# Expert sums of a decoder step: picked rows gathered per token in place of dense scoring and summing

## The reference, cut to what matters

```python
q = (hx @ w_pq).reshape(PEER_BLOCK, PEER_HEADS, 2, PK_HALF)
s = jnp.einsum('nhpc,hpkc->nhpk', q, sub_keys).astype(jnp.float32)
top_s, top_i = lax.top_k(s, PEER_TOPK)
cand = top_s[:, :, 0, :, None] + top_s[:, :, 1, None, :]
best_s, best = lax.top_k(cand.reshape(PEER_BLOCK, PEER_HEADS, PEER_TOPK * PEER_TOPK), PEER_TOPK)
i1 = jnp.take_along_axis(top_i[:, :, 0, :], best // PEER_TOPK, axis=-1)
i2 = jnp.take_along_axis(top_i[:, :, 1, :], best % PEER_TOPK, axis=-1)
eidx = i1 * N_KEYS + i2
g = jax.nn.softmax(best_s, axis=-1).astype(hx.dtype)
a = jax.nn.gelu(jnp.einsum('nd,nhkd->nhk', hx, expert_u[eidx]), approximate=False) * g
return jnp.einsum('nhk,nhkd->nd', a, expert_v[eidx])
```

## Time and profile before

| | us |
|---|---|
| timed runs, median of 3 | 5564.8 |
| lowest and highest of them | 5531.41, 5573.28 |
| span of the profiled execution | 5573.4 |
| its mean granted TensorE clock | 0.937 of 2.4 GHz |

### The profile page before, as it was taken

The page is one execution under the profiler, slowest core; times in us unless marked ns, Lnnn a source line. Parts: engine busy times, 40 slices in busy tenths (PEclk is TensorE's granted clock), DMA queues, the critical chain, the costliest instruction groups (busy, mean ns, idle before and its releaser), DMA issues. The chain is left out here.

```text
span 5573.4 us, 84134 instructions
## 1 busy us (share of the span) xinstructions
PE 5087.3 (91%) x30108; PEld 4765.7 (86%) x30108; DVE 3082.1 (55%) x8353; ACT 1509.8 (27%) x2813; POOL 210.5 (4%) x226
## 2 busy tenths in 40 slices
PE   7798899999289969899999979999999999999998
PEld 5474578898278869799999979999999999999998
DVE  1664434333511238899888867777644444444444
ACT  1364323222201122222455532211111122111111
POOL 0000001000000000000000012222100000000000
PEclk9899798969679989999999999999999999999999
DMA  3001003121411121122344365555422222222222
GB/s 122 5 1 40 35 20 107 65 73 46 161 48 46 61 95 39 42 84 84 122 178 172 154 186 137 136 136 136 118 69 72 71 68 72 68 68 70 70 75 81
DMA packets 405688, 477.91 MB, mean 86 GB/s; under 512 B 311106, under 2 KB 320714, under 8 KB 402002
## 3 DMA queue, kind: packets, MB, share of 16 engines
q1 hardware_dynamic: 380818, 374.17, 22.0%
q10 hardware_dynamic: 18736, 65.20, 3.4%
q0 software_dynamic: 5904, 35.65, 1.9%
HBM read 353.17 MB, written 121.80 MB: 85 GB/s over the span
## 5 line engine op out<-in xcount | busy, mean ns | idle before, releaser
L173 PE MATMUL bank<-ex_a_high,ex_v_high 128*128 128x344 f32 x3072 | 982.7, 320 | 24.5 <-DVE ex_v_low L180 21.3
L174 PE MATMUL bank<-ex_a_low,ex_v_high 128*128 128x344 f32 x3072 | 985.9, 321 | 0.0
L175 PE MATMUL bank<-ex_a_high,ex_v_low 128*128 128x344 f32 x3072 | 979.7, 319 | 0.0
L2153 DVE TENSOR_TENSOR experts_out<-experts_out,bank 128x344 f32<-128x344 f32 x1536 | 761.6, 511 | 362.9 <-PE bank L175 361.8
L173 PE MATMUL bank<-h_high,ah_u_high 128*128 128x344 f32 x1824 | 599.2, 328 | 72.2 <-DVE ah_u_low L180 72.2
L173 PEld LDWEIGHTS bank<-ex_a_high,ex_v_high 128*128 128x128 f32 x3072 | 578.4, 188 | 32.4 <-DVE ex_v_low L180 22.1
L175 PE MATMUL bank<-h_high,ah_u_low 128*128 128x344 f32 x1824 | 587.5, 322 | 0.0
L174 PE MATMUL bank<-h_low,ah_u_high 128*128 128x344 f32 x1824 | 587.0, 322 | 0.0
L175 PEld LDWEIGHTS bank<-ex_a_high,ex_v_low 128*128 128x128 f32 x3072 | 577.7, 188 | 0.0
L174 PEld LDWEIGHTS bank<-ex_a_low,ex_v_high 128*128 128x128 f32 x3072 | 577.4, 188 | 0.0
L173 PE MATMUL bank<-h_high,ex_u_high 128*128 128x344 f32 x1632 | 521.2, 319 | 1.9 <-DVE ex_u_low L180 1.9
(11 more groups left out here) (357 smaller groups left out, 8602.7 us busy)
## 6 DMA issues: line engine op xcount, KB each, us to landing
gates_dram<-gt_stage SPq DMA_DIRECT2D x16, 4096.0 KB, 12.6
ex_g<-gates_dram SPq DMA_DIRECT2D x128, 512.0 KB, 4.7
ex_v<-in_v SPq DMA_DIRECT2D x128, 512.0 KB, 3.6
ex_u<-in_uT SPq DMA_DIRECT2D x68, 512.0 KB, 4.1
gelu_dram<-ah_gelu ACTq DMA_DIRECT2D x60, 516.0 KB, 2.9
ex_u<-gelu_dram SPq DMA_DIRECT2D x60, 516.0 KB, 3.8
ah_u<-in_uT ACTq DMA_DIRECT2D x60, 512.0 KB, 3.9
d_w<-in_w_dil POOLq DMA_DIRECT2D x9, 2048.0 KB, 8.5
```

Source lines behind the costliest of these rows:

```text
L173: pe.matmul(out, w[0], x[0], start=start, stop=False)
L174: pe.matmul(out, w[0], x[1], start=False, stop=False)
L175: return pe.matmul(out, w[1], x[0], start=False, stop=stop)
L2153: dve.tensor_tensor(at, at, YB[n % NB][:, 0:CH], ALU.add).then_inc(s["y"], 1)
```

## The change

`Ahead`, `stage_gates`, `stage_experts` and `stage_output` go, with their scratch tensors. `stage_norm` leaves h2 in full float32 in `c.h2` as well (in the tile that held its input). `stage_route` ends after the 16 best of each half. The host lays `expert_u` and `expert_v` side by side in one table, `uv`, of 16384 rows of 2048 float32 (8192 bytes).

A new `stage_peer` does the rest, in tiles of 128 tokens, with tokens on partitions. Class `Picks` has the code of the pick from `stage_route` in three parts (`best_pairs`, `indices`, `finish`) and ends in one expert number and one gate per token and pick. A *gather* is one indirect DMA issued by POOL: 128 rows of `uv`, one per token. Four gathers make a *batch* (G), 32 batches a tile of tokens, 2 batches hold all of the 8 sample tokens (16 partitions each): 258 batches, 1032 gathers. The ring of row tiles holds three batches (RB). Core of the diff:

```diff
-    c.ps = [ctx.enter_context(nc.psum_tensor(f"bank{i}", [P, 512], F32)) for i in range(8)]
+    c.psum = ctx.enter_context(nc.psum_tensor("banks", [P, 8, 512], F32))
+    c.ps = [c.psum[:, i] for i in range(8)]
...
-        x = sb("x", [P, KD, TOK])
+        x = c.h2 if parts else sb("x", [P, KD, TOK])
...
+            @block.gpsimd
+            def _(pool):
+                for B, (t, b) in enumerate(batches):
+                    if b == 0 and t < LAST:
+                        pool.wait_ge(pk.done, t + 1)
+                    elif b == 0:
+                        pool.wait_ge(s["tail_in"], 32)
+                    if B >= RB:
+                        pool.wait_ge(s["sum"], B - RB + 1)
+                    picks = pick_t if t == LAST else pk.expert[t % 2]
+                    for j in range(G):
+                        r = B % RB * G + j
+                        at = picks[:, b * G + j:b * G + j + 1]
+                        pool.indirect_dma_start(out=rows[r][:, :], out_offset=None, in_=IN["uv"][:, :],
+                                                in_offset=bass.IndirectOffsetOnAxis(ap=at, axis=0))\
+                            .then_inc(rows_in[r], 16)
...
+                for B, (t, b) in enumerate(batches):
...
+                    for j in range(G):
+                        r = B % RB * G + j
+                        dve.wait_ge(rows_in[r], 16 * uses(B, j))
+                        h = H[t % 2].rearrange("p a b -> p (a b)")
+                        ins = dve.tensor_tensor_reduce(rows[r][:, 0:D], rows[r][:, 0:D], h, 1.0, 0.0, ALU.mult, ALU.add,
+                                                       dots[:, B % RB, j:j + 1])
+                    ins.then_inc(s["dot"], 1)
+                    if B:
+                        gates(B - 1)
+                    if t < LAST:
+                        if b == 4:
+                            pk.best_pairs(dve, t + 1)
+                        if b == 8:
+                            pk.indices(dve, t + 1)
+                        if b == 12:
+                            pk.finish(dve, t + 1)
+                        if b == 6 and t:
+                            add_out(t - 1)
...
+                def diags(B):
...
+                    act.wait_ge(s["gate"], B + 1)
+                    if B >= DB:
+                        act.wait_ge(s["sum"], B - DB + 1)
+                    for j in range(G):
+                        ins = act.activation(diag[:, B % DB, j, 0:w], base[:, 0:w], ACT.Copy,
+                                             scale=a[:, B % RB, j:j + 1])
+                    ins.then_inc(s["diag"], 1)
...
+                for B, (t, b) in enumerate(batches):
+                    act.wait_ge(s["dot"], B + 1)
+                    act.activation(act_of[:, B % RB], dots[:, B % RB], ACT.Gelu).then_inc(s["gelu"], 1)
+                    if B:
+                        diags(B - 1)
...
+                for B, (t, b) in enumerate(batches):
+                    n = TILES[t][1]
+                    if b == 0 and t:
+                        turn_out(t - 1)
+                        if t + 1 < NT:
+                            h_rows(t + 1)
+                    pe.wait_ge(s["diag"], B + 1)
+                    for j in range(G):
+                        r = B % RB * G + j
+                        ends = dict(start=(b == 0 and j == 0), stop=(B + 1 == first[t + 1] and j == G - 1))
+                        for half in range(2):
+                            ins = pe.matmul(A[half][0:n, :], diag[:, B % DB, j, 0:n],
+                                            rows[r][:, D + half * 512:D + (half + 1) * 512], **ends)
+                    ins.then_inc(s["sum"], 1)
```

More of the change, by code:

```diff
@@ L1592, in _ @@
                         w_low(dve, KD + m + 1)
[L1595 to L1656, removed]
@@ L1676, in stage_route @@
         sc2 = sb("sc_rest", [P, NT, NK])
[L1677 to L1689, removed]
+        s = {n: c.sem("rt_" + n) for n in "keys_in w_hi w_lo mm copy sc_mm sc_copy top".split()}
         w_in = [c.sem(f"rt_w_in{i}") for i in range(2)]
@@ L1724, in _ @@
                             ins.then_inc(s["sc_mm"], 1)
[L1725 to L1734, removed]
             @block.scalar
@@ L1770, in _ @@
                                .then_inc(s["sc_copy"], 1)
[L1771 to L1789, removed]
             @block.vector
@@ new lines, in stage_peer, with uses @@
+def stage_peer(c):
+    nc, IN, OUT = c.nc, c.IN, c.OUT
+    NT = len(TILES)
+    LAST = NT - 1
+    G, RB = 4, 3
+    RS = G * RB
+    DB = 2
+    PER = PH * TOPK // G
+    TAILB = PH * TOPK * NSA // P // G
+    batches = [(t, b) for t in range(NT) for b in range(TAILB if t == LAST else PER)]
+    first = [batches.index((t, 0)) for t in range(NT)] + [len(batches)]
+    with ExitStack() as ctx:
+        sb = lambda t, shape, dt=F32: ctx.enter_context(nc.sbuf_tensor("pe_" + t, shape, dt))
+        pk = Picks(c, ctx)
+        rows = [sb(f"rows{i}", [P, 2 * D]) for i in range(RS)]
+        dots = sb("dots", [P, RB, G])
+        act_of = sb("gelu", [P, RB, G])
+        a = sb("a", [P, RB, G])
+        diag = sb("diag", [P, DB, G, P])
+        out = sb("out", [P, D])
+        x1 = [sb(f"x1_{i}", [P, KD, P]) for i in range(2)]
+        ts = sb("tail_y", [P, KD, NSA])
+        h_tail = sb("h_tail", [NSA, D])
+        owner = sb("owner", [NSA, P])
+        ownerT = sb("ownerT", [P, NSA])
+        pick_t = sb("pick_tail", [P, TAILB * G], U32)
+        gate_t = sb("gate_tail", [P, TAILB * G])
+        rows_in = [c.sem(f"pe_rows_in{i}") for i in range(RS)]
+        x_in = [c.sem(f"pe_x_in{i}") for i in range(2)]
+        stored = [c.sem(f"pe_stored{i}") for i in range(2)]
+        s = {n: c.sem("pe_" + n) for n in ("small_in tail_out tail_in h ht htc dot gelu gate diag sum accc "
+                                           "turn y").split()}
+        H = [c.psum[:, 0:2], c.psum[:, 2:4]]
+        A, Y = c.ps[4:6], c.ps[6:8]
+        gate2 = c.mod[:, 5]
+        def uses(b, r):
+            return (b * G + r) // RS + 1
@@ new lines, in _, with copy_out @@
+            @block.scalar
+            def _(act):
+                def copy_out(t):
+                    n = TILES[t][1]
+                    act.wait_ge(s["sum"], first[t + 1])
+                    if t:
+                        act.wait_ge(s["turn"], t)
+                    for half in range(2):
+                        ins = act.activation(out[0:n, half * 512:(half + 1) * 512], A[half][0:n, :], ACT.Copy)
+                    ins.then_inc(s["accc"], 1)
+                def diags(B):
+                    t, b = batches[B]
+                    base = ownerT if t == LAST else c.ident
+                    w = NSA if t == LAST else P
+                    act.wait_ge(s["gate"], B + 1)
[5 more added lines that the diff above has]
+                    ins.then_inc(s["diag"], 1)
+                act.wait_ge(s["small_in"], 32)
+                pk.exps(act, 0)
+                act.wait_ge(s["ht"], 1)
+                for half in range(2):
+                    ins = act.activation(h_tail[:, half * 512:(half + 1) * 512], Y[half][0:NSA, :], ACT.Copy)
+                ins.then_inc(s["htc"], 1)
+                for B, (t, b) in enumerate(batches):
[3 more added lines that the diff above has]
+                        diags(B - 1)
+                    if b == 6 and t < LAST:
+                        pk.exps(act, t + 1)
+                    if b == 1 and t:
+                        copy_out(t - 1)
+                diags(len(batches) - 1)
+                copy_out(LAST)
@@ L2322, in build_program @@
+                turn_out(LAST)
 def build_program(nc, IN, OUT, upto=99, dbg=None):
```

637 lines of the change are left out of this document (176 added, 461 removed).

## The result

The changed kernel takes 5921.14 us (median of 3, 5913.84 to 5933.1) against 5564.8: 1.064 of the time before, 95% interval 1.059 to 1.069. It is slower where I forecast 5350 us and faster, and it lies outside my range of 5020 to 5780. Its profiled execution has a span of 5919.3 us, 569 above the forecast.

What follows compares the result with a forecast made beforehand. PE bounded the old expert stage; the new one would be a loop limited by its short ring. Start 2319 + 3, first pick 33, landing 5, loop 2786, picks 168, tile changes 24, end 12: 5350 us, range 5020 to 5780.

Steps and rivals of the forecast that it cites:

- eight matmuls 5.2: PE's sums in the new loop: eight float32 matmuls of 512 columns a batch at 0.65 us each, 5.2 us.
- The kernel before was bound by PE, and its first 2319 us stay: Old kernel: PE alone bounds the experts' work from 2319 to 5546 us; norm and key search before it stay unchanged.
- Transfers, 2.48 us a gather: DMA in the new loop: each 1.0486 MB gather takes 2.48 us at 423 GB/s, 9.9 us a batch.
- POOL 0.9 to 1.3, hidden: POOL in the new loop: an indirect issue takes 0.9 to 1.3 us, hidden except for a batch's first.
- DVE 1.25 with the read-out: DVE in the new loop: a dot product takes 1.25 us with the sum's read-out, 5.0 a batch.
- The ring of three gives back a batch too late, and two batches cost the path plus one batch of transfers: New loop: 11.7 us from a batch's landing to B+2's first bytes, plus 9.9 of transfers: 21.6 for two batches.
- The picks, 168: Eight later picks between batches on DVE: 21 us a tile remain, 168 us in all.
- PE at the middle of the clock: PE's bursts in the new loop: a clock between 1.2 and 2.4 GHz, 0.65 us a matmul.
- A: Rival on the new loop: PE keeps full clock, 3.6 us a batch, ending at 5029 us; chance 0.15.
- B: Rival on the new loop: PE at 1.2 GHz throughout, matmuls 7.1 us a batch, ending at 5596; chance 0.12.
- C: Rival on the DMA engines: scattered rows move at 337 GB/s, 12.4 us a batch, ending at 5745; chance 0.17.
- D: Rival on POOL: an indirect issue costs 3.5 us, so POOL bounds the kernel, ending at 6008; chance 0.11.

Runs made afterwards that it cites:

- Experiments 1 and 11: Against the changed kernel: 1 sums only half of the columns, 5513.6 us; 11 makes the sums in float32r from a fixed tile, 5297.31 us.
- experiment 2: Changed kernel without the eight later picks, all tiles using the first tile's picks and gates: 5809.61 us.
- experiment 8: Changed kernel with row tiles freed on landing, dots and sums reading other data, and plain loads of 128 consecutive rows replacing the gathers: 4969.28 us.
- experiment 3: Changed kernel with gates and identities issued right behind their own batch's dots, not the next one's: 5162.56 us, 0.9288 of the kernel before.
- experiment 7: Changed kernel with row tiles freed on landing, gathers still scattered, dots and sums reading other data: 4966.49 us.
- experiment 6: Changed kernel with batches of two gathers, six in the ring, and each pick cut into 18 steps: 4976.87 us, 0.8931 of the kernel before.

## Why the prediction was wrong

**The failed step** is one term of the sum, "eight matmuls 5.2", that is 8 × 0.65. I took "Eight plain float32 matmuls of 512 columns took 3.78 us" from the earlier trace rows, where the row says x8. That x8 counts records, and a call of plain float32 leaves two. So that row was four calls; a batch's eight calls are sixteen records, 7.13 us at the full clock, and 9.37 in the path with the clock as it was. The trace of before could have told. Its row for a product whose calls can be counted in the code, at L422 (two groups of 3 chunks by 8 steps, 48 calls):

```profile
L422 PE MATMUL bank<-hT,mp_w_q x96: 452/452/939, 111.7 to 140.7; 128*128 128x344 f32 x96
```

96 records for 48 calls. I even wrote "2064 for gates" in "What goes", though L1906 is called once per token, 1032 times, and didn't ask why. The float32r row has one record per call: x3072 for 128 tiles of 24. The doubling belongs to products, not to all that PE does in float32: the transposes at L1993 of the changed kernel are 9 × 8 calls and 72 records. The Trainium skill has a sentence I did not weigh: "FP8 and Floating Point Precision", "TensorE Precision Notes", says that true FP32 takes four passes through the array. The trace agrees: 0.43 us per record and 2.4 GHz are some 1030 cycles for 512 columns, two to a column, four with both records. Experiments 1 and 11 show the doubling to be the format's: half the calls leave half the records, still two each, and the same number of calls in float32r leaves one each.

**The account of the missed 569 us.** The pair took 26.37 us against 21.6, 4.77 more. Of it PE's burst is 9.37 − 5.2 = 4.17; issue and landings are (5.43 + 8.61) − (3.3 + 9.9) = 0.84; the small links 0.25 less. Over 129 pairs: 538 + 108 − 32 = 614. The picks were 57 under their term (experiment 2). 614 − 57 = 557, and 12 us are left over; they were not traced further. The turn of 26.37 us is one turn taken from the trace, so the account is good to some tens of us.

**By its steps:**

- *The kernel before was bound by PE, and its first 2319 us stay.* Right: from 2060 to 2319 us PE is busy 223.18 us against 221.89, DVE 194.53 against 192.72.
- *Transfers, 2.48 us a gather.* Right: dots that follow one another at 2.48 us (2781.30 to 2783.79), and 421 GB/s when nothing holds them.
- *POOL 0.9 to 1.3, hidden.* Right, 0.94 and 0.30 until the next. That it "can't be below 0.88" was no floor: the plain issue of this shape took 0.53 (experiment 8).
- *DVE 1.25 with the read-out.* Right, 1.22 and 0.08.
- *The ring of three gives back a batch too late, and two batches cost the path plus one batch of transfers.* Right in form. Ring of two, gates at once and smaller batches all move the time as this formula says. This was the costliest property of the kernel: 759 us with one edit, 859 with another.
- *The picks, 168.* Too high; 111.
- *PE at the middle of the clock.* Right that both levels occur, but 0.65 us for each was too slow a mean: 2135.2 / 4128 = 0.52 us over the stage, and 9.37 / 16 = 0.59 in the burst on the path. With the right count that term would have been 16 × 0.65 = 10.4 us, 1.0 too long; so this error hid a part of the miscount.

**The rivals.** *A* needed PE's eight calls in 3.6 us and falls with the same miscount: they took 7.13 us at the full clock. *B* (1.2 GHz throughout) is not what happened: the stage's clock is 0.78, and a burst that starts 0.55 or 1.33 us behind the last takes 7.13 us while one behind 8.67 us of rest takes 9.37. By the rule that it leaned on, the Trainium skill's "TensorE: Matmul & The Clock Gate", "HAM oscillation — how this bites in real kernels", every burst behind a wait for DMA starts at the low clock: the trace agrees for the long rests (4.5 us and more in experiments 1 and 11, 8.67 in the changed kernel, where the first records of the burst lie 0.86 us apart). For short ones it is mixed: behind 2.80 us, less than the waits in the page's own case, experiment 3 has one burst of 7.13 us and one of 8.80. What decides between the two was not found. *C* (scattered rows are slow) is refuted by experiments 7 and 8, and with it the 358 GB/s of the Trainium skill's "DMA: Bandwidth & Descriptors", "Where 436 GB/s comes from", for this one core running alone: here it moved 421, and the measurement decides. *D* (POOL the bound) is refuted by 0.94 us an issue; the 102 cycles per index of the Trainium skill's "GPSIMD Engine Reference", "Performance pitfalls for Q7 kernels", would have made 10.9 us of it, an estimate, and don't apply to this indirect DMA.

**The range** was too narrow for the same reason: it took PE's row as known and varied only the clock on it. None of the cases had twice the records. With them the middle case itself ends near the result: path 8.4 + 5.2 = 13.6, the cycle (13.6 + 3.3 + 9.9)/2 = 13.4, 258 × 13.4 = 3457, and the sum 6021, against a span of 5919.3. That it comes within 102 us is in part luck, since the too long burst (1.0 us × 129) and the picks (57) stand against landings that took 108 longer.

## What to carry to other kernels

Before a row of the trace prices a new operation, count the calls in the code that made the row: a plain float32 product was two records here, and "x8" was four calls. In a stage where no engine is full, write the loop of waits out and ask first what holds the buffers: giving them back one batch earlier, or in smaller batches from the same memory, was worth 759 and 859 us here, more than the cut of PE's work to half (407) or its sums in float32r (624). When the transfers are gapless (DMA share 1.0, 416 to 421 GB/s) neither order nor batch size has more to give: experiment 6 stands 10 us above experiment 7, and what is left is the number of bytes.

## What was not expected of the hardware

- A matmul call of plain float32 is two MATMUL records, 0.86 us for 512 columns at the full clock; one of float32r is one record, and eight of them took 3.78 us even at the lower clock. A float32 transpose is one record.
- Less work for PE lowered its clock: with half the sums the stage's clock fell from 0.78 to 0.70, with float32r to 0.57, and with added work it rose to about 0.9. Half the records took 5.7 to 6.6 us, where all of them had taken 9.37.
- Scattered rows of 8192 bytes move at the full 421 GB/s, like plain loads; the indirect issue costs POOL 0.94 us and 0.30 until the next, where the plain one costs 0.53.
